# Moving the SBUF buffers of a two-model fp32 kernel: starts at multiples of 64 bytes, and different offsets modulo 512 bytes

## The chip, the cores and the metric

The kernel runs on one core of one Trainium2 chip. The metric is the device time of one execution in microseconds; the median of three runs is given for the kernel before.

## What is computed

Two small transformer-like blocks are run one after the other on one sequence of 512 tokens with 1024 channels, all in fp32. Cut to what matters, each of the linear layers is `h @ w` with 1024 (or 2816) rows of weights:

```python
for layer in range(2):                       # first block
    h = rmsnorm(x, attn_norm[layer])
    x = x + (even_mixer if layer == 0 else odd_mixer)(h, ...)   # projections, attention, output projection
    x = x + conv_glu_ffn(rmsnorm(x, ffn_norm[layer]), ...)      # 1024 -> 2 x 2816 -> 1024
x = rmsnorm(x, final_norm)
for i in range(2):                           # second block
    h = _rmsnorm(x, norm_g) * (1 + scale) + shift
    proj = h @ w_in                          # queries, keys, indexer, gates, state-space inputs
    merged = sigmoid(gl_att) * y_att + sigmoid(gl_ssd) * y_ssd
    x = x + gate * (merged @ w_out)
return rmsnorm(x, final_g)
```

## The kernel before, in words

Activations lie transposed in SBUF: 128 channels on the partitions, 512 tokens along the free axis, so a vector of 1024 channels is 8 tiles of 128 x 512 fp32 (2048 bytes in each partition). `xT` is the residual stream, `hT` the normalised input of a layer, and `arena` is one large buffer from which every stage takes its temporaries by an `Area`, in whole numbers of words from the arena's start. `arena_r` and `hv_r` are the same memory as `arena` and `hv`, seen as the type that TensorE reads in one pass (F32R).

**Linear layers.** To keep fp32 accuracy, a weight tile and an activation tile are each split into a high part and a low part, and a product is made of three matmuls: high by high, high by low, low by high (`pe_linear_steps`, `pe_pair`; all recorded at line 458 in the helper `mm`). A matmul is 128 x 128 weights (the stationary operand, loaded by a weight load of its own) by 128 x 512 activations (the moving operand). The weights arrive in panels of eight tiles, 512 KB each: SP moves panel after panel into the five slots of `ring`. ACT copies a panel's high part into one of three slots of `wparts` (line 566), then DVE, or POOL for some panels, subtracts and writes the low part (line 570). This is `keep_up`, which each engine calls in its own program so that it stays two panels ahead of TensorE; `tile_of` gives TensorE the next weight tile and waits for the low part. A slot of `wparts` is written again when TensorE has finished the panel three back, a slot of `ring` when its low part is made.

The activation operand of a linear layer is either `hT` (its high and low halves) or a pair of tiles in the arena: the attention output, the gated hidden channels of the feed-forward layer, the state-space output and the merged gates are split there by ACT (line 596) and DVE (line 600). The bf16 matmuls of `pe_busy` (line 533, recorded at 458) only keep TensorE working while a norm is computed.

**Order.** Each engine has its own program; semaphores tie them. The order of the matmuls is written out by hand, and nothing in it depends on an address.

**Where the buffers lie.** Buffers are laid one behind the other, each rounded up to 32 bytes in a partition. The first, `ring`, begins at byte 16512. From the sizes, before and after the change (the byte within a partition, then that byte modulo 64 and modulo 512):

| buffer | before | mod 64 | mod 512 | after | mod 64 | mod 512 |
|---|---|---|---|---|---|---|
| ring | 16512 | 0 | 128 | 16896 | 0 | 0 |
| wparts slots 0, 1, 2 | 36992, 45184, 53376 | 0 | 128, 128, 128 | 37376, 45632, 54016 | 0 | 0, 64, 256 |
| xT | 61568 | 0 | 128 | 62208 | 0 | 256 |
| hT high, low | 77952, 94336 | 0 | 128, 128 | 78592, 95040 | 0 | 256, 320 |
| hv, rot, vecs | 110720, 118912, 123008 | 0 | 128 | 111424, 119616, 123712 | 0 | 320 |
| cf_sb | 125088 | 32 | 160 | 125824 | 0 | 384 |
| cb_sb | 128928 | 32 | 416 | 129664 | 0 | 128 |
| small, rstd, arena | 131040, 132064, 136160 | 32 | 480 | 131776, 132800, 136896 | 0 | 192 |

`vecs` has 517 columns, 2068 bytes, which take 2080; that is what puts everything behind it at 32 modulo 64. The tiles that the linear layers read in the arena begin at multiples of 64 bytes from its start, so in the kernel before they lie at 480 or at 32 modulo 512.

Of the kernel before, what the change touches and what calls it, by code (L numbers as in the profile page):

```python
# [8 lines left out]
F32 = mybir.dt.float32  # L9
F32R = mybir.dt.float32r  # L10
BF16 = mybir.dt.bfloat16
ALU = mybir.AluOpType
ACT = mybir.ActivationFunctionType
AX = mybir.AxisListType

P = 128
D = 1024
KD = D // P
SEQ = 512
# [13 lines left out]
RAW = 5  # L33
PARTS = 3
# [106 lines left out]
def vec_layout():  # L141
    at, n = {}, 0
    for name, layer, cols in (
        [("attn_norm", l, KD) for l in range(2)] + [("ffn_norm", l, KD) for l in range(2)]
        + [("conv_w", (l, j), FC) for l in range(2) for j in range(3)] + [("conv_b", l, FC) for l in range(2)]
        + [("final_norm", 0, KD), ("pos_k", 0, CMP_LEN), ("pos_v", 0, CMP_LEN), ("b_f", 0, 1), ("c", 0, KD)]
        + [("b_ada", l, 24) for l in range(2)] + [("norm_g", l, KD) for l in range(2)]
        + [("xconv_w", (l, j), 12) for l in range(2) for j in range(4)] + [("xconv_b", l, 12) for l in range(2)]
        + [("dt_bias", l, 1) for l in range(2)] + [("a_log", l, 1) for l in range(2)]
        + [("d_skip", l, KD) for l in range(2)] + [("ssm_g", l, KD) for l in range(2)] + [("final_g", 0, KD)]  # L150
    ):
        at[name, layer] = n
        n += cols
    return at, n


VEC, NVEC = vec_layout()
# [89 lines left out]
def finish(steps):  # L247

    if isinstance(steps, STEPS_TYPE):
        for _ in steps:  # L250
            pass
# [102 lines left out]
def build(nc, ins, out, known=None, final=False):  # L354
    stream_of, x_in, vec_in, cf_in, cb_in, rot_in = ins
# [8 lines left out]
    with ExitStack() as ctx:  # L364
        def sb(name, shape, dt=F32):
            return ctx.enter_context(nc.sbuf_tensor(name, shape, dt))

        ring = sb("ring", [P, RAW, KD, P])
        wparts = sb("wparts", [P, PARTS, 2, KD, P], F32R)
        xT = sb("xT", [P, KD, SEQ])  # L370
        hT = sb("hT", [P, 2, KD, SEQ], F32R)
        hv = sb("hv", [P, 4, SEQ])
        hv_r = nc.alloc_sbuf_tensor_at("hv_r", [P, 4, SEQ], F32R, offset=nc.sbuf_base - 16 * SEQ)
        rot = sb("rot", [P, 2, SEQ])
        vec = sb("vecs", [P, NVEC])
        cf = sb("cf_sb", [P, NCF])
        cb = sb("cb_sb", [P, NCB], BF16)
        small = sb("small", [P, 256])
# [24 lines left out]
        vec_landed = ctx.enter_context(nc.semaphore("vec_landed"))  # L403
# [69 lines left out]
        def landed(eng, panel):  # L473
            eng.wait_ge(panel_landed[panel % RAW], 16 * (panel // RAW + 1))

        def tile_of(pe):

            while kinds[tile_no[0] // KD] == "DVE":
                tile_no[0] += KD
            t = tile_no[0]  # L480
            tile_no[0] += 1
            panel, j = divmod(t, KD)
            ends = panel if j == KD - 1 else None
            if kinds[panel] == "split":
                if j == 0:
                    pe.wait_ge(*(pool_made if panel in lo_on_pool else dve_made)["w_lo", panel])
                slot = place[panel] % PARTS
                return (wparts[:, slot, 0, j, :], wparts[:, slot, 1, j, :]), ends
            if j == 0:
                landed(pe, panel)  # L490
            return ring[:, panel % RAW, j, :], ends
# [6 lines left out]
        def pe_linear_steps(pe, key, n, rhs, rows, ready, pool=ALL_BANKS):  # L498

            bank = banks.take(pe, (key, n), pool)  # L500
            for k in range(rows):
                (hi, lo), ends = tile_of(pe)
                if ready:
                    pe.wait_ge(*ready(k))
                last = k == rows - 1
                mm(pe, bank[:, :], lhsT=hi, rhs=rhs[:, 0, k, :], start=(k == 0), stop=False)
                mm(pe, bank[:, :], lhsT=hi, rhs=rhs[:, 1, k, :], start=False, stop=False)
                mm(pe, bank[:, :], lhsT=lo, rhs=rhs[:, 0, k, :], start=False, stop=last,
                   done=(key, n) if last else None, ends=ends)
                if k in (2, 5):  # L510
                    yield
            banks.panel_of[key, n] = (tile_no[0] - 1) // KD

        def pe_pair(pe, keys, rhs, ready, busy=0):
            taken = [banks.take(pe, key) for key in keys]
            pe_busy(pe, taken[0], busy)
            first = tile_no[0]
            for k in range(KD):
                pe.wait_ge(*ready(k))
                for m, (key, bank) in enumerate(zip(keys, taken)):  # L520
                    tile_no[0] = first + KD * m + k
                    (hi, lo), ends = tile_of(pe)
                    last = k == KD - 1
                    mm(pe, bank[:, :], lhsT=hi, rhs=rhs[:, 0, k, :], start=(k == 0), stop=False)
                    mm(pe, bank[:, :], lhsT=hi, rhs=rhs[:, 1, k, :], start=False, stop=False)
                    mm(pe, bank[:, :], lhsT=lo, rhs=rhs[:, 0, k, :], start=False, stop=last,
                       done=key if last else None, ends=ends)
            for m, key in enumerate(keys):
                banks.panel_of[key] = first // KD + m
# [19 lines left out]
        def keep_up(eng, who, key, ahead=PARTS - 1):  # L549

            if banks.last_panel is None:
                return
            end = banks.last_panel[key]
            upto = place[end] + ahead
            while split_at[who] <= min(upto, len(splits) - 1):
                i = split_at[who]
                p = splits[i]
                if any(k != "split" for k in kinds[end + 1:max(end, p - RAW) + 1]):
                    return
                split_at[who] += 1  # L560
                slot = i % PARTS
                if who == "act":
                    landed(eng, p)
                    if i >= PARTS:
                        eng.wait_ge(*filled["panel", splits[i - PARTS]])
                    eng.activation(wparts[:, slot, 0, :, :], ring[:, p % RAW, :, :], ACT.Copy)\  # L566
                       .then_inc(*act_made.mark(("w_hi", p)))
                elif (who == "pool") == (p in lo_on_pool):
                    eng.wait_ge(*act_made["w_hi", p])
                    eng.tensor_tensor(wparts[:, slot, 1, :, :], ring[:, p % RAW, :, :],  # L570
                                      wparts[:, slot, 0, :, :].bitcast(F32), ALU.subtract)\
                       .then_inc(*(pool_made if who == "pool" else dve_made).mark(("w_lo", p)))

        HALF = slice(0, DH), slice(DH, P)
# [2312 lines left out]
        @block.sync  # L2887
        def _(sp):
            for t in range(NT):
                sp.dma_start(x_nat[:, t, :], x_in[t * P:(t + 1) * P, :]).then_inc(x_landed[t], 16)  # L2890
            for i in range(n_panels):
                if i >= RAW:
                    old = i - RAW
                    kind = kinds[old]
                    lo_made = pool_made if old in lo_on_pool else dve_made
                    sp.wait_ge(*(lo_made["w_lo", old] if kind == "split" else filled["panel", old] if kind == "PE"
                                 else dve_made["ada panel", old]))
                sp.dma_start(ring[:, i % RAW, :, :].rearrange("p k w -> p (k w)"), stream_of[i])\
                  .then_inc(panel_landed[i % RAW], 16)
                if i == 1:  # L2900
                    sp.dma_start(cf[:, P:NCF], cf_in[:, P:NCF]).then_inc(cf_landed, 16)
                if i == 2:
                    sp.dma_start(cb[:, :], cb_in).then_inc(cb_landed, 16)
                    sp.dma_start(rot[:, :, :].rearrange("p a b -> p (a b)"), rot_in[:, 0:2 * SEQ]).then_inc(rot_landed, 16)

            sp.wait_ge(*dve_made["y last"])
            for t in (0, 2, 1, 3):
                sp.wait_ge(*(act_made if t < 2 else dve_made)["y", t])
                sp.dma_start(out[t * P:(t + 1) * P, :], y_nat[:, t, :]).then_inc(out_stored, 16)
            sp.wait_ge(out_stored, 16 * NT)  # L2910

        @block.scalar
        def _(act):
            act.dma_start(cf[:, 0:P], cf_in[:, 0:P]).then_inc(ident_landed, 16)
            act.dma_start(vec[:, :], vec_in).then_inc(vec_landed, 16)
            for part in prog["act"]:
                finish(part(act))

# [93 lines left out]
```

## Time and profile before

| | |
|---|---|
| median of 3 runs | 2462.91 us (2462.30 to 2463.08) |
| profiled execution, span from the first to the last instruction | 2462.0 us |
| TensorE matmuls | 12086, busy 97% of the span |
| of these, 128 x 512 by weights in `wparts` | 5520 + 48 with hT as the moving operand, 2400 with the arena |
| DVE, ACT, POOL busy | 58%, 41%, 11% |
| mean granted TensorE clock | 0.990 |

The profiled execution's own time beyond the span is not given; its span lies 0.9 us under the median of the runs. Busy time of TensorE is the union of the matmuls' intervals; since they are pipelined, the mean duration of one (some 390 ns) is longer than the distance from one start to the next. That distance is had from a merged stretch of the timeline: (its length minus the duration of the last one) divided by the count minus one.

### The profile page before, as it was taken

The page shows a single profiled execution, that of the slowest core. Times are in us where ns is not written, and L with a number is a line of the kernel's source. Part 1 is how long each engine was busy: PE and PEld are TensorE (multiplying, and loading weights), DVE is VectorE, ACT ScalarE, POOL GpSimd, SP SyncE. Part 2 cuts the span into 40 slices and gives each one's busy share as a digit, 9 for nine tenths or more (in the row PEclk, how much of TensorE's full clock was granted, in tenths as well). Part 3 has the DMA queues.
Part 4 walks back from the last instruction along what each step waited for, and adds up shares of the span by engine and source line. Part 5 has one row for each costly group of instructions (what it writes and reads, how often), then busy time and mean ns, then how long its engine had stood idle before and what let it go on. Part 6 is the DMA issues. An engine that isn't in the chain of part 4 may idle for free.

```text
span 2462.0 us, 32019 instructions
## 1 busy us (share of the span) xinstructions
PE 2394.7 (97%) x12086; PEld 1926.7 (78%) x12086; DVE 1423.4 (58%) x2366; ACT 1019.3 (41%) x1732; POOL 273.9 (11%) x260
## 2 busy tenths in 40 slices
PE   8999899999999999999999999989999999999998
PEld 7877788888887888788888866767888777678886
DVE  3545665655655666566556469947533578666333
ACT  3666664322334444443233334444422354445223
POOL 0000111000000000100000236302100233011001
PEclk8999999999999999999999999999999999999999
DMA  4311002433432111133433312101222221102321
GB/s 180 111 52 44 1 27 95 153 122 128 151 123 87 66 54 61 52 120 130 146 127 137 112 65 73 61 35 38 94 99 91 78 74 60 43 27 78 103 95 52
DMA packets 58039, 211.77 MB, mean 86 GB/s; under 512 B 6432, under 2 KB 6560, under 8 KB 57888
## 3 DMA queue, kind: packets, MB, share of 16 engines
q1 hardware_dynamic: 57456, 208.86, 23.9%
q8 instruction: 99, 1.62, 0.3%
q10 hardware_dynamic: 432, 0.85, 0.1%
q14 instruction: 52, 0.43, 0.1%
HBM read 207.60 MB, written 2.10 MB: 85 GB/s over the span
## 4 chain that ended last, share of the span: by engine, by line
PE 84%; DVE 6%; issue 4%; ACT 3%; POOL 1%; DMA 0%; SPq 0%; ACTq 0%; DVEq 0%; POOLq 0%
PE bank L458 77%; PE last_bank L458 5%; PE bank L468 3%; DVE arena L1145 1%; DVE arena L2232 1%; DVE arena L2234 1%; DVE small L831 1%; ACT arena L819 1%; ACT wparts L566 1%; POOL rstd L625 0%; DMA cb_sb<-cb_dram 0%; DVE wparts L570 0%; DVE arena L2567 0%; DVE arena_r L584 0%; DVE arena L1006 0%
## 5 line engine op out<-in xcount | busy, mean ns | idle before, releaser
L458 PE MATMUL bank<-hT,wparts 128*128 128x512 f32 x5520 | 1335.8, 398 | 5.2 <-DMA cb_sb<-cb_dram 3.6
L458 PEld LDWEIGHTS bank<-hT,wparts 128*128 128x128 f32 x5520 | 1034.2, 190 | 237.4 <-issue 23.2
L570 DVE TENSOR_TENSOR wparts<-ring,wparts 128x1024 fp32r<-128x1024 f32 x290 | 366.7, 1265 | 427.1 <-ACT wparts L566 426.9
L458 PE MATMUL bank<-arena_r,wparts 128*128 128x512 f32 x2400 | 566.1, 396 | 0.0
L458 PEld LDWEIGHTS bank<-arena_r,wparts 128*128 128x128 f32 x2400 | 450.0, 188 | 108.5 <-DVE arena_r L600 0.3
L566 ACT ACTIVATE wparts<-ring 128x1024 fp32r<-128x1024 f32 x332 | 348.2, 1049 | 163.8 <-PE bank L458 132.6
L819 ACT ACTIVATE arena<-bank,small 128x128 f32<-128x128 f32 (+3 forms) x192 | 100.9, 526 | 143.4 <-DVE small L831 142.2
L468 PE MATMUL bank<-cf_sb,arena 128*128 128x128 f32 (+1 forms) x816 | 131.5, 278 | 14.9 <-DMA cf_sb<-cf_dram 5.2
L458 PE MATMUL last_bank<-arena 128*128 128x64 f32 x972 | 131.5, 271 | 8.6 <-DVE arena L854 4.4
L458 PEld LDWEIGHTS last_bank<-arena 128*128 128x128 f32 x972 | 122.6, 193 | 17.6 <-issue 11.4
L831 DVE TENSOR_REDUCE small<-bank 128x1 f32<-128x128 f32 (+3 forms) x192 | 93.3, 486 | 57.1 <-PE bank L458 55.0
L570 POOL TENSOR_TENSOR wparts<-ring,wparts 128x1024 fp32r<-128x1024 f32 x42 | 101.1, 2410 | 212.1 <-ACT wparts L566 212.0
L468 PEld LDWEIGHTS bank<-cf_sb,arena 128*128 128x128 f32 (+1 forms) x816 | 95.6, 146 | 30.6 <-DMA cf_sb<-cf_dram 5.2
L596 ACT ACTIVATE arena_r<-arena 128x512 fp32r<-128x512 f32 x68 | 42.9, 632 | 179.9 <-POOL arena L2791 93.7
L625 POOL TENSOR_TENSOR rstd<-hv 128x512 f32<-128x512 f32 x6 | 7.8, 1297 | 939.8 <-ACT hv L615 939.8
L458 PE MATMUL bank<-arena 128*64 128x128 f32 (+6 forms) x708 | 91.6, 330 | 14.0 <-ACT arena L819 13.5
L811 ACT ACTIVATE arena<-bank 128x384 f32<-128x384 f32 (+3 forms) x136 | 58.0, 426 | 110.5 <-PE bank L468 109.7
L1136 ACT ACTIVATE arena<-arena,vecs 128x512 f32<-128x512 f32 x44 | 36.0, 817 | 147.2 <-DVE arena L1821 147.2
L458 PEld LDWEIGHTS bank<-arena 128*128 128x128 f32 (+2 forms) x708 | 63.4, 170 | 29.6 <-ACT arena L819 16.2
L1145 DVE SCALAR_TENSOR_TENSOR arena<-arena,vecs 128x511 f32<-128x511 f32 x88 | 66.0, 750 | 16.7 <-ACT arena L1136 15.1
L458 PE MATMUL bank<-cb_sb 128*128 128x128 bf16 (+2 forms) x377 | 73.9, 253 | 0.0
L1821 DVE TENSOR_TENSOR arena<-bank,rstd 128x512 f32<-128x512 f32 x44 | 30.4, 691 | 66.5 <-PE bank L458 62.1
(277 smaller groups left out, 2125.5 us busy)
## 6 DMA issues: line engine op xcount, KB each, us to landing
ring<-weights_dram SPq DMA_DIRECT2D x388, 512.0 KB, 3.3
arena<-x_dram SPq DMA_DIRECT2D x4, 512.0 KB, 6.1
out_dram<-arena SPq DMA_DIRECT2D x4, 512.0 KB, 4.0
rot<-rot_dram SPq DMA_DIRECT2D x1, 512.0 KB, 10.9
rot<-rot_dram ACTq DMA_DIRECT2D x1, 512.0 KB, 3.0
cf_sb<-cf_dram SPq DMA_DIRECT2D x1, 416.0 KB, 9.3
cb_sb<-cb_dram SPq DMA_DIRECT2D x1, 264.0 KB, 10.1
vecs<-vec_dram ACTq DMA_DIRECT2D x1, 258.5 KB, 6.1
```

What stands on the lines that cost most here:

```text
L458: i = pe.matmul(*args, **kw)
L468: i = pe.transpose(*args)
L566: eng.activation(wparts[:, slot, 0, :, :], ring[:, p % RAW, :, :], ACT.Copy)\
L570: eng.tensor_tensor(wparts[:, slot, 1, :, :], ring[:, p % RAW, :, :], wparts[:, slot, 0, :, :].bitcast(F32), ALU.subtract)\
L596: act.activation(dst, src, ACT.Copy).then_inc(*act_made.mark((key, "hi")))
L811: act.activation(PT[:, j % 3, 0:W], banks[key, "t", j][:, 0:W], ACT.Copy)\
L819: act.activation(Pb[:, i % 3, 0:W], banks[key, "s", i][:, 0:W], ACT.Exp, bias=mx(i), accum_out=sm(i)).then_inc(*act_made.mark((key, "p", i)))
L831: dve.tensor_reduce(mx(i), banks[key, "s", i][:, 0:W], AX.X, ALU.max, negate=True)\
L1136: act.activation(cv, src, ACT.Identity, bias=b, scale=w).then_inc(*act_made.mark((key, "tap", n)))
L1145: dve.scalar_tensor_tensor(out=cv[:, s:SEQ], in0=src[:, 0:SEQ - s], scalar=w, in1=cv[:, s:SEQ], op0=ALU.mult, op1=ALU.add)\
L1821: dve.tensor_tensor(an[:, n % 3, :], banks[(key, "a"), n][:, :], scale, ALU.mult)\
L2232: dve.max(tops[:, r, :], sc).then_inc(*dve_made.mark((K + "top", qt, r)))
```

## The change

It puts padding buffers ahead of `ring`, ahead of the second and third slot of `wparts` (which become three buffers) and between the two halves of `hT` (which become two buffers in a `Pair`, indexed as before), and rounds `vecs` up to 528 columns. The padding is never read or written. No instruction is added or removed, no shape, no order and no wait is changed; the DMA into `vecs` writes the same 517 columns.

```diff
--- before.py
+++ after.py
@@ -365,14 +365,21 @@
         def sb(name, shape, dt=F32):
             return ctx.enter_context(nc.sbuf_tensor(name, shape, dt))
 
+        sb("pad_ring", [P, 96])
         ring = sb("ring", [P, RAW, KD, P])
-        wparts = sb("wparts", [P, PARTS, 2, KD, P], F32R)
+        wparts = []
+        for i in range(PARTS):
+            if i:
+                sb(f"pad_w{i}", [P, (0, 16, 48)[i]])
+            wparts.append(sb(f"wparts{i}", [P, 2, KD, P], F32R))
         xT = sb("xT", [P, KD, SEQ])
-        hT = sb("hT", [P, 2, KD, SEQ], F32R)
+        hi_of_h = sb("hT_hi", [P, KD, SEQ], F32R)
+        sb("pad_h", [P, 16])
+        hT = Pair(hi_of_h, sb("hT_lo", [P, KD, SEQ], F32R))
         hv = sb("hv", [P, 4, SEQ])
         hv_r = nc.alloc_sbuf_tensor_at("hv_r", [P, 4, SEQ], F32R, offset=nc.sbuf_base - 16 * SEQ)
         rot = sb("rot", [P, 2, SEQ])
-        vec = sb("vecs", [P, NVEC])
+        vec = sb("vecs", [P, (NVEC + 15) // 16 * 16])
         cf = sb("cf_sb", [P, NCF])
         cb = sb("cb_sb", [P, NCB], BF16)
         small = sb("small", [P, 256])
@@ -485,7 +492,7 @@
                 if j == 0:
                     pe.wait_ge(*(pool_made if panel in lo_on_pool else dve_made)["w_lo", panel])
                 slot = place[panel] % PARTS
-                return (wparts[:, slot, 0, j, :], wparts[:, slot, 1, j, :]), ends
+                return (wparts[slot][:, 0, j, :], wparts[slot][:, 1, j, :]), ends
             if j == 0:
                 landed(pe, panel)
             return ring[:, panel % RAW, j, :], ends
@@ -563,12 +570,12 @@
                     landed(eng, p)
                     if i >= PARTS:
                         eng.wait_ge(*filled["panel", splits[i - PARTS]])
-                    eng.activation(wparts[:, slot, 0, :, :], ring[:, p % RAW, :, :], ACT.Copy)\
+                    eng.activation(wparts[slot][:, 0, :, :], ring[:, p % RAW, :, :], ACT.Copy)\
                        .then_inc(*act_made.mark(("w_hi", p)))
                 elif (who == "pool") == (p in lo_on_pool):
                     eng.wait_ge(*act_made["w_hi", p])
-                    eng.tensor_tensor(wparts[:, slot, 1, :, :], ring[:, p % RAW, :, :],
-                                      wparts[:, slot, 0, :, :].bitcast(F32), ALU.subtract)\
+                    eng.tensor_tensor(wparts[slot][:, 1, :, :], ring[:, p % RAW, :, :],
+                                      wparts[slot][:, 0, :, :].bitcast(F32), ALU.subtract)\
                        .then_inc(*(pool_made if who == "pool" else dve_made).mark(("w_lo", p)))
 
         HALF = slice(0, DH), slice(DH, P)
@@ -2912,7 +2919,7 @@
         @block.scalar
         def _(act):
             act.dma_start(cf[:, 0:P], cf_in[:, 0:P]).then_inc(ident_landed, 16)
-            act.dma_start(vec[:, :], vec_in).then_inc(vec_landed, 16)
+            act.dma_start(vec[:, 0:NVEC], vec_in).then_inc(vec_landed, 16)
             for part in prog["act"]:
                 finish(part(act))
 
```

## Rows read from the trace of the kernel before

**Rows 1.** The page: span, busy time by engine, PE's slices and its granted clock
```profile
span 2462.0 us, 32019 instructions
...
PE 2394.7 (97%) x12086; PEld 1926.7 (78%) x12086; DVE 1423.4 (58%) x2366; ACT 1019.3 (41%) x1732; POOL 273.9 (11%) x260
...
PE   8999899999999999999999999989999999999998
...
PEclk8999999999999999999999999999999999999999
```

**Rows 2.** The page: the chain that ended last, by engine and by line
```profile
PE 84%; DVE 6%; issue 4%; ACT 3%; POOL 1%; DMA 0%; SPq 0%; ACTq 0%; DVEq 0%; POOLq 0%
PE bank L458 77%; PE last_bank L458 5%; PE bank L468 3%; DVE arena L1145 1%; DVE arena L2232 1%; DVE arena L2234 1%; DVE small L831 1%; ACT arena L819 1%; ACT wparts L566 1%; POOL rstd L625 0%; DMA cb_sb<-cb_dram 0%; DVE wparts L570 0%; DVE arena L2567 0%; DVE arena_r L584 0%; DVE arena L1006 0%
```

**Rows 3.** Groups of PE matmuls, shapes apart: busy us, mean ns | idle before
```profile
L458 PE MATMUL bank<-hT,wparts 128*128 128x512 f32 x5520 | 1335.8, 398 | 5.2 <-DMA cb_sb<-cb_dram 3.6 <-DVE arena L1145 0.9 <-POOL wparts L570 0.6
L458 PE MATMUL bank<-arena_r,wparts 128*128 128x512 f32 x2400 | 566.1, 396 | 0.0
L458 PE MATMUL last_bank<-arena 128*128 128x64 f32 x972 | 131.5, 271 | 8.6 <-DVE arena L854 4.4 <-DVE arena L857 0.9 <-ACT arena L811 0.6
...
L458 PE MATMUL last_bank<-hT,wparts 128*128 128x512 f32 x48 | 12.9, 411 | 0.0
```

**Rows 4.** Timeline of PE, 1797 to 1848: start, us to last end, instructions
```profile
1797.24 11.06 PE L458 MATMUL bank<-hT,wparts 128*128 128x512 f32 x48
1808.14 11.38 PE L458 MATMUL bank<-arena_r,wparts 128*128 128x512 f32 x48
1819.35 11.05 PE L458 MATMUL bank<-hT,wparts 128*128 128x512 f32 x48
1830.24 5.76 PE L458 MATMUL bank<-arena_r,wparts 128*128 128x512 f32 x24
1835.84 11.06 PE L458 MATMUL bank<-hT,wparts 128*128 128x512 f32 x48
```

**Rows 5.** Timeline of PE, a long stretch with a right operand in the arena
```profile
1176.51 61.78 PE L458 MATMUL bank<-arena_r,wparts 128*128 128x512 f32 x264
```

**Rows 6.** Timeline of PE, back-to-back bf16 matmuls of 512 columns
```profile
1423.07 3.41 PE L458 MATMUL bank<-cb_sb 128*128 128x512 bf16 x15
```

**Rows 7.** Timeline of PE, a short run inside the third stage (forgetting attention)
```profile
906.20 1.78 PE L458 MATMUL bank<-hT,wparts 128*128 128x512 f32 x7
```

**Rows 8.** Tile wparts, PE and its weight loads: ns min/median/max
```profile
L458 PEld LDWEIGHTS bank<-hT,wparts x5520: 186/188/333, 15.1 to 2396.6; 128*128 128x128 f32 x198
...
L458 PEld LDWEIGHTS bank<-arena_r,wparts x2400: 186/188/192, 350.8 to 2449.7; 128*128 128x128 f32 x185
...
L458 PE MATMUL bank<-hT,wparts x5520: 387/389/796, 15.1 to 2396.8; 128*128 128x512 f32 x198
...
L458 PE MATMUL bank<-arena_r,wparts x2400: 388/394/482, 350.8 to 2450.0; 128*128 128x512 f32 x185
```

**Rows 9.** Tile arena_r, PE: matmuls with weights in the arena
```profile
L458 PE MATMUL bank<-arena_r x160: 222/337/481, 243.8 to 999.5; 128*128 128x128 f32 x40, 128*128 128x256 f32 x40, 128*128 128x384 f32 x40, 128*128 128x512 f32 x40
L458 PE MATMUL bank<-hv_r,arena_r x64: 221/336/741, 72.1 to 235.7; 128*128 128x128 f32 x16, 128*128 128x256 f32 x16, 128*128 128x384 f32 x16, 128*128 128x512 f32 x16
```

**Rows 10.** Groups of ACT and DVE instructions, shapes apart (two answers, ACT first)
```profile
L566 ACT ACTIVATE wparts<-ring 128x1024 fp32r<-128x1024 f32 x332 | 348.2, 1049 | 163.8 <-PE bank L458 132.6 <-DMA ring<-weights_dram 31.2
L596 ACT ACTIVATE arena_r<-arena 128x512 fp32r<-128x512 f32 x68 | 42.9, 632 | 179.9 <-POOL arena L2791 93.7 <-DVE arena L1830 86.2
...
L615 ACT ACTIVATE hv<-xT 128x512 f32<-128x512 f32 x48 | 29.9, 623 | 92.1 <-DVE xT L2852 31.1 <-DVE xT L1116 30.9 <-DVE xT L1112 30.1
...
L570 DVE TENSOR_TENSOR wparts<-ring,wparts 128x1024 fp32r<-128x1024 f32 x290 | 366.7, 1265 | 427.1 <-ACT wparts L566 426.9
L1732 DVE SCALAR_TENSOR_TENSOR arena<-ring,small,arena 128x1024 f32<-128x1024 f32 x42 | 53.7, 1279 | 0.0
```

**Rows 11.** Who waited for whom: us in total, times, longest us
```profile
DVE wparts L570 <- ACT wparts L566: 426.9, 263, 5.3
...
ACT wparts L566 <- PE bank L458: 132.6, 43, 4.6
...
ACT wparts L566 <- DMA ring<-weights_dram: 31.2, 7, 12.2
```

**Rows 12.** The page: DMA issues, KB each, median us to landing
```profile
ring<-weights_dram SPq DMA_DIRECT2D x388, 512.0 KB, 3.3
...
vecs<-vec_dram ACTq DMA_DIRECT2D x1, 258.5 KB, 6.1
```

## The prediction

> **What bounds the kernel now.** I read the page first. TensorE has a matmul in flight for 97% of the span, and no slice of the 40 falls far below that; the granted clock reads 8 tenths in the first slice and 9 (90% or more of 2.4 GHz) in every other [rows 1]. The chain that ended last is TensorE's for 84% of the span, DVE has 6%, ACT 3% and DMA 0% [rows 2]. So only what shortens or lengthens matmuls counts in full. Next the groups by shape: three quarters of TensorE's busy time is one kind of instruction, 128 x 512 activations against a 128 x 128 weight tile from `wparts`: 5520 + 48 of them with `hT` moving, 2400 with the arena moving [rows 3]. The mean durations (398 and 396 ns) hide the difference that matters here, because they hold the pipeline's latency and, for hT, stretches with interruptions. The timeline shows it. In one stage of the second model the two kinds alternate in equal stretches: 48 matmuls on hT take 11.06 us from first start to last end, 48 on the arena take 11.38 [rows 4]. Take off the duration of the last, 389 and 394 ns [rows 8], and divide by 47: **227.0 ns from start to start on hT, 233.7 on the arena**. The long stretch says the same: (61.78 - 0.39) / 263 = 233.4 ns [rows 5]. Same weights' buffer, same shape, same type, no idle time; what differs is where the moving operand lies: hT at 0 modulo 64, the arena at 32 modulo 64, by the address table.
>
> 512 columns at 2.4 GHz are 213.3 ns. The bf16 filler matmuls come near: (3.41 - 0.38) / 14 = 216.4 ns [rows 6], with 0.38 for the duration of one [rows 3]. They also lie at 32 modulo 64 and pay nothing visible, but they read half the bytes in the same time. So the fp32 stream at one column a cycle seems to be at the edge of what its reads deliver. In round numbers the two are 544 and 560 cycles at 2.4 GHz, 226.7 and 233.3 ns, which I use from here; the difference of 16 cycles, 6.67 ns, is the time of 16 columns, that is of 64 bytes. A row of 2048 bytes at 32 modulo 64 touches 33 pieces of 64 bytes, an aligned one 32. That fits one extra piece for each arena matmul; it is an inference, the trace shows no addresses.
>
> **The change part by part.**
>
> *The arena at a multiple of 64.* 2400 matmuls go from 233.3 to 226.7 ns: 2400 x 6.67 = **16.0 us** less. All of it is on TensorE's chain: the group has 0.0 us of idle time before it [rows 3]. The cover that must hold is the making of weight parts. A panel is 24 matmuls, 24 x 226.7 = 5.4 us (5.6 before on the arena); in it DVE needs 1.27 us and ACT 1.05 for the parts [rows 10], and the next panel lands in 3.3 us [rows 12]. DVE and ACT wait for each other and for TensorE, hardly for the DMA, 31.2 us in seven waits [rows 11]. So nothing is late next, and I charge 0; if the cover went, the price would be at most the 0.2 us a panel that was gained, 100 arena panels x 0.2 = 16 us, the whole gain.
>
> *Other matmuls that read the arena or cf_sb.* TensorE's other busy time is 2394.7 - 1335.8 - 566.1 - 12.9 = 480 us [rows 1, 3]. Most are two-instruction fp32 products or short ones, the largest 972 of 64 columns, 131.5 us [rows 3]; they don't read at the full rate. The one-pass products with weights in the arena give the nearest direct comparison: with `arena_r` moving (misaligned) the minimum and median are 222 and 337 ns, with `hv_r` moving (aligned) 221 and 336 [rows 9], a difference of 1 ns; but there the weights are misaligned in both, and the runs are three matmuls long. Bounds: 0, and 480 x 6.7 / 226.7 = 14 us if all of it scaled as the arena stretches do. By the nearest row, 1 ns in 337, I take 1.5 us.
>
> *ACT, DVE, POOL.* ACT's copy of 512 columns takes 632 ns from and to the arena, and a square from xT to hv, both aligned, 623; DVE's two-source operation of 1024 columns takes 1279 in the arena and 1265 on ring and wparts [rows 10]. The operations differ too, so 1 to 1.5% is the upper bound of the gain from alignment. They are on the chain for 9% of the span, 222 us [rows 2]: 0 to 3 us, I take 1. Off the chain it is hidden by TensorE.
>
> *hT and the weights.* They are aligned already. What the change moves is the distance between the two streams that TensorE reads at once, the moving rows and the next weights (a weight load takes 188 ns of the 227, so it runs beside the matmul [rows 8]). Before, hT and every weight slot are both at 128 modulo 512, distance 0; the arena is at a distance of 352 or 416. After, the distance is 256 or 320, 192 or 256, and 0 or 64, for the three slots. The trace of before has no aligned pair at a distance other than 0. The bounds: at best the excess over the bf16 distance of 216.4 vanishes, 227 to 216.4 ns, 5568 x 10.6 = 59 us on hT and 2400 x 10.3 = 25 us more on the arena; at worst distance 0 is what makes hT cheap, and hT goes to the arena's 233.4, 5568 x 6.7 = 37 us lost. There is also a middle: in short runs the distance is not settled, (1.78 - 0.39) / 6 = 231.7 ns in a run of seven [rows 7], against 227.0 in long ones [rows 4]; the same addresses, so something of the two streams' timing matters. I take 0: the arena's excess over hT is explained by one piece of 64 bytes at distances of 352 and 416, with nothing left over for the distance, so the value nearest to the rows is no effect.
>
> The page on TensorE of the Trainium skill ("TensorE: Matmul & The Clock Gate", Part 2) says that the engine has two independent read ports, and that loading the next weights steals nothing from the running matmul. By it the distance is worth nothing in either direction, as I took it; 227 against 216.4 ns is not explained by it.
>
> *Padding, vecs, DMA.* 736 bytes more in a partition; no engine works on them. The panel DMAs have the same packets and a destination 384 bytes further, hidden by the ring's depth; the vecs DMA lands the same bytes in 6.1 us [rows 12]. 0.
>
> The sum: 16.0 + 1.5 + 1 = 18.5 us less. 2462.0 - 18.5 = 2443.5 as a span; with the 0.9 us by which the median of the runs stands above it, **2444.4 us**.
>
> **The rivals.**
>
> 1. *The distance matters and gets better* (chance 0.25). For: the 11 ns above the bf16 rate, and the unsettled 231.7 ns [rows 4, 6, 7]. Against: distances of 0, 352 and 416 show the same once the extra piece is taken off. Price: half of the excess, 5 ns for 7968 matmuls, is 40 us on top: 2404. The full excess gives 2444 - 84 = 2360. Nearer ones, such as all runs settling at 226.7, give 5 to 10 us, 2437.
>
> 2. *Distance 0 was the cheap place* (chance 0.17; slower). The trace can't tell "aligned" from "at the same offset modulo 512 as the weights", since hT has both and the arena neither. If the second is what gives 227 ns, all 5568 hT matmuls go towards 233.4, and the arena stays: 2463 + 37 = 2500. If alignment is right and the distance costs as well, say as in the unsettled run, hT goes to 231.7 for + 5568 x 4.7 = 26 us, the arena gains 4: 2485. It decides from a loss of 2.9 ns for each hT matmul on (16 / 5568). Against: at 352 and 416, two different distances, the arena's excess is the same, and it is just one piece of 64 bytes.
>
> 3. *Nothing changes* (chance 0.12). If the reads are made in pieces smaller than 64 bytes, 32 modulo 64 is no misalignment and the 6.7 ns come from something that stays, as the place in the arena or the way its tiles follow each other. Then 2462. The hv_r against arena_r rows, 1 ns apart [rows 9], speak for it; the two clean levels of rows 4 and 5 speak against it, with nothing else between them. The page "SBUF — State Buffer" of the Trainium skill (Door 1, the note on cachelines) gives lines of 16 bytes; by it a start at 32 modulo 64 costs nothing, so this is the result it would have. No row shows such lines.
>
> **How the numbers follow.** Forecast as worked out, 0.46; rivals 0.25, 0.17, 0.12. Its own range is 2430 to 2447: with the upper bounds of the other matmuls and engines (14 and 3 us for 1.5 and 1) it is 2430, with neither 2447. The range of 8 in 10 takes in rival 3 and the likelier half of rival 1, to 2404, and the first 5 us of rival 2: 2404 to 2468; left out are the rest of rival 2 and the deeper half of rival 1, with the weight nearer 0.04 there. A measurement of this kernel can tell 0.2%, 4.9 us, from no change. Faster by more than that: 0.46 + 0.25 = 0.71. Within: rival 3, and 0.01 of rival 2 in which its loss just balances the gain, 0.13. Slower: the rest of rival 2, 0.16.
>
> **What would show it.** Right: the stretches of 48 arena matmuls [rows 4] take 11.06 us, the stretch of 264 takes 60.0 instead of 61.78, hT stretches still 11.06. Rival 1: hT stretches of 48 below 10.9 us. Rival 2: hT stretches at 11.2 to 11.38. Rival 3: both as before. ACT's 632 ns going to 623 would show the third term by itself. I would be wrong in kind if the three weight slots came out different from one another, panel by panel, for then the distance counts and the mean hides it.

## The result, and the profile after

The changed kernel takes **2478.75 us** (median of 4 runs, 2477.25 to 2479.52) against 2462.61 for the kernel before; the ratio is 1.0065, with a 95% interval of 1.0053 to 1.0077. It is 16 us slower where 18.5 us faster was forecast, and lies outside the stated range of 2404 to 2468.

The page of the changed kernel, span, busy time, clock and chain (it answers to [rows 1, 2]):

```profile
span 2476.7 us, 32007 instructions
...
PE 2408.3 (97%) x12074; PEld 1921.2 (78%) x12086; DVE 1424.0 (57%) x2366; ACT 1019.8 (41%) x1732; POOL 273.9 (11%) x260
...
PEclk9999999999999999999999999999999999999999
...
PE 83%; DVE 7%; issue 4%; ACT 4%; POOL 1%; DMA 0%; SPq 0%; ACTq 0%; DVEq 0%; POOLq 0%
```

TensorE still bounds the kernel, with 13.6 us more of busy time; DVE, ACT and POOL have what they had. (The trace holds 12 matmul records fewer, all of bf16 matmuls on `cb_sb`; the program has the same matmuls.) The groups of matmuls by shape (busy us, mean ns | idle before); hT is now two buffers, whose intervals overlap, so their busy times can't be added:

```profile
L465 PE MATMUL bank<-hT_hi,wparts 128*128 128x512 f32 x3680 | 1221.2, 403 | 5.1 <-ACT hT_hi L700 4.2 <-DVE rstd L2353 0.4 <-DVE hT_lo L745 0.4
L465 PE MATMUL bank<-hT_lo,wparts 128*128 128x512 f32 x1840 | 729.1, 396 | 0.0
L465 PE MATMUL bank<-arena_r,wparts 128*128 128x512 f32 x2400 | 561.9, 394 | 0.0
```

Against [rows 3], 2400 arena matmuls take 561.9 us instead of 566.1. The high half of hT has 403 ns for the mean of one, the low half 396, 398 before for both. The timeline, in the stage of [rows 4] (of the hT stretches the first row alone stands here, since the two halves alternate):

```profile
1805.21 5.71 PE L465 MATMUL bank<-arena_r,wparts 128*128 128x512 f32 x24
1810.76 0.40 PE L465 MATMUL bank<-hT_hi,wparts 128*128 128x512 f32 x1
...
1821.90 11.18 PE L465 MATMUL bank<-arena_r,wparts 128*128 128x512 f32 x48
1832.91 0.39 PE L465 MATMUL bank<-hT_hi,wparts 128*128 128x512 f32 x1
...
1844.09 5.66 PE L465 MATMUL bank<-arena_r,wparts 128*128 128x512 f32 x24
```

A stretch on hT lasts from its first start to the start of the arena stretch behind it: 1821.90 - 1810.76 = 11.14 us for 48, **232.1 ns**, and 1844.09 - 1832.91 = 11.18, 232.9. In [rows 4] the same was 1808.14 - 1797.24 = 10.90, 227.1. The arena stretches went from 11.38 to 11.18 and from 5.76 to 5.71 and 5.66. And the long one, [rows 5] 61.78 us:

```profile
1182.95 61.66 PE L465 MATMUL bank<-arena_r,wparts 128*128 128x512 f32 x264
```

(61.66 - 0.39) / 263 = 233.0 ns: it lies at a multiple of 64 now and has gained 0.4 ns of the 6.7. Where the forecast had 60.0 us, nearly nothing happened. The tiles' rows (duration ns min/median/max, first and last start), which answer to [rows 8], show the loss in the durations as well:

```profile
L465 PE MATMUL bank<-hT_hi,wparts x3680: 387/395/803, 14.8 to 2412.2; 128*128 128x512 f32 x194
...
L465 PE MATMUL bank<-arena_r,wparts x2400: 387/394/483, 347.7 to 2464.6; 128*128 128x512 f32 x185
...
L465 PE MATMUL bank<-hT_lo,wparts x1840: 387/396/632, 15.1 to 2411.9; 128*128 128x512 f32 x184
```

The median on hT was 389 ns and is 395 and 396, the arena's is 394 as it was. From the first to the last arena matmul it was 2099.2 us and is 2116.9.

To see which matmuls pay, I took each distance from one start to the next out of the trace, for all consecutive pairs of 128 x 512 matmuls with weights in `wparts`, and averaged those up to 262 ns (longer ones hold a wait, or ran at the lower of the two granted clocks, 1.2 GHz). The trace has no addresses: each matmul's come from the kernel's program, whose order of matmuls is the trace's. A pair is counted by its earlier matmul, and the distance from weight to moving operand is taken modulo 256:

```
                                 count, after   before    after
hT                                      5115    227.9    232.6
  slot 0 (after: 0 high, 64 low)        1633    227.8    231.9
  slot 1 (after: 192 high, 0 low)       1848    227.9    233.8
  slot 2 (after: 0 high, 64 low)        1634    227.9    231.9
arena                                   2377    233.5    231.7
  after, tiles at distance 0             563              228.4
  after, tiles at distance 128           416              232.3
  after, tiles at distance 192          1398              232.8
```

5100 x 4.7 = 24 us are lost on hT and 2380 x 1.8 = 4.3 gained on the arena: 20 us at 2.4 GHz, where the two spans differ by 14.7. The rest is the clock. The two profiled executions did not have the same:

```profile
core 0: 2462.0 us, clock 0.990
```

```profile
core 0: 2476.7 us, clock 0.992
```

By the trace, the kernel before was at 1.2 GHz for 48.3 us of its span and the changed one for 37.5. Of the pairs on hT, 73 ran at 1.2 GHz before, at 430 ns in the mean, and 37 after. Those that were longer than 262 ns at 2.4 GHz, which are the ones with a wait, sum to 75.8 us before and 75.9 after, so no part of the loss went into waits. At 430 ns instead of 228 a stretch does about half the work: 10.8 / 2 = 5.4 us came back, an estimate, and 20 - 5.4 = 14.6.

The other terms of the sum: ACT and the waits around the weight parts (two views; they answer to [rows 10, 11]):

```profile
L603 ACT ACTIVATE arena_r<-arena 128x512 fp32r<-128x512 f32 x68 | 42.9, 631 | 178.7 <-POOL arena L2798 92.6 <-DVE arena L1837 86.2
...
L622 ACT ACTIVATE hv<-xT 128x512 f32<-128x512 f32 x48 | 29.9, 624 | 90.6 <-DVE xT L2859 30.5 <-DVE xT L1119 30.1 <-DVE xT L1123 30.1
```

```profile
DVE wparts L577 <- ACT wparts L573: 431.0, 263, 5.6
...
ACT wparts L573 <- PE bank L465: 131.3, 41, 4.8
...
ACT wparts L573 <- DMA ring<-weights_dram: 31.4, 6, 12.7
```

ACT's 632 ns in the arena are 631, 623 are 624: alignment to 64 bytes gives ACT nothing.

### The profile page after: what moved, and what is told of

It reads as the page before. It is cut to its first block, busy times and chain, and to the rows that moved or that the text cites. A ratio compares the mean times of both kernels' runs of the same rounds, so it can differ in the third digit from the quotient of the medians.

```text
span 2476.7 us, 32007 instructions
## 1 busy us (share of the span) xinstructions
PE 2408.3 (97%) x12074; PEld 1921.2 (78%) x12086; DVE 1424.0 (57%) x2366; ACT 1019.8 (41%) x1732; POOL 273.9 (11%) x260
## 4 chain that ended last, share of the span: by engine, by line
PE 83%; DVE 7%; issue 4%; ACT 4%; POOL 1%; DMA 0%; SPq 0%; ACTq 0%; DVEq 0%; POOLq 0%
PE bank L465 76%; PE last_bank L465 4%; PE bank L475 3%; DVE arena L1152 1%; DVE arena L2239 1%; DVE arena L2241 1%; ACT wparts L573 1%; DVE small L838 1%; ACT arena L826 1%; POOL rstd L632 0%; DVE arena L2574 0%; DVE wparts L577 0%; DMA ring<-weights_dram 0%; ACT arena L2147 0%; DVE arena L2226 0%
## 5 line engine op out<-in xcount | busy, mean ns | idle before, releaser
L465 PE MATMUL bank<-hT_hi,wparts 128*128 128x512 f32 x3680 | 1221.2, 403 | 5.1 <-ACT hT_hi L700 4.2
L465 PEld LDWEIGHTS bank<-hT_hi,wparts 128*128 128x128 f32 x3680 | 695.5, 189 | 180.0 <-issue 16.6
L465 PE MATMUL bank<-hT_lo,wparts 128*128 128x512 f32 x1840 | 729.1, 396 | 0.0
L465 PE MATMUL bank<-arena_r,wparts 128*128 128x512 f32 x2400 | 561.9, 394 | 0.0
L465 PEld LDWEIGHTS bank<-hT_lo,wparts 128*128 128x128 f32 x1840 | 348.0, 189 | 78.5 <-issue 6.2
L475 PE MATMUL bank<-cf_sb,arena 128*128 128x128 f32 (+1 forms) x816 | 129.9, 276 | 14.7 <-DMA cf_sb<-cf_dram 5.0
L465 PEld LDWEIGHTS last_bank<-arena 128*128 128x128 f32 x972 | 124.0, 195 | 16.9 <-issue 10.6
L465 PE MATMUL bank<-arena 128*64 128x128 f32 (+6 forms) x708 | 92.0, 331 | 14.1 <-ACT arena L826 13.6
```

Source lines behind the costliest of these rows:

```text
L465: i = pe.matmul(*args, **kw)
L475: i = pe.transpose(*args)
```

## The experiments

Three theories stood after this. **D**: what is cheap is a moving operand at the same offset, modulo 256 or 512, as the weights (rival 2 of the prediction, in general form). **A**: alignment to 64 bytes, as forecast, with something else lost on top. **O**: the place in SBUF. All kernels are the kernel before with padding (e8 and e11 also move tiles inside the arena), except e9, which is the changed kernel with one padding moved. Beside them the kernel before had medians of 2462.8 to 2463.0 us. The bytes of padding behind a moved buffer bring those after it back to their offset modulo 512. "ns" is the mean distance from start to start as above. The last column is the span times the mean granted clock of each execution, the median of them: an estimate of the span had the clock been 2.4 GHz throughout. It is there because the mean clock was between 0.9895 and 0.993 from kernel to kernel, and 0.001 of it is 2.5 us.

| run | hT to weights, mod 256 | arena to weights, mod 256 | hT ns | arena ns | median us | ratio to before, 95% | span x clock, us |
|---|---|---|---|---|---|---|---|
| before | 0 | 96, 160 | 227.9 | 233.5 | 2462.6 | | 2435 to 2437 |
| after | see above | see above | 232.6 | 231.7 | 2478.75 | 1.0053 to 1.0077 | 2456.1 |
| e1_arena_equal | 0 | 0, 64 | 227.9 | 229.0 | 2452.39 | 0.9935 to 0.9969 | 2426.3 |
| e2_round64 | 0 | 128, 192 | 227.9 | 232.6 | 2459.60 | 0.9976 to 0.9995 | 2435.8 |
| e3_h_low_64 | 0 high, 64 low | 96, 160 | 231.9 | 233.4 | 2478.69 | 1.0047 to 1.0077 | 2458.4 |
| e4_w_64 | 192 | 32, 96 | 233.2 | 233.2 | 2485.60 | 1.0076 to 1.0106 | 2464.8 |
| e5_w_128 | 128 | 224, 32 | 232.5 | 233.3 | 2482.92 | 1.0058 to 1.0090 | 2460.0 |
| e6_w_256 | 0 (256) | 96, 160 | 227.9 | 233.5 | 2462.34 | 0.9984 to 1.0002 | 2437.9 |
| e7_all_misaligned | 0 | 0, 64 | 227.9 | 229.0 | 2453.12 | 0.9943 to 0.9971 | 2425.8 |
| e8_all_equal | 0 | 0 | 227.8 | 226.9 | 2447.69 | 0.9920 to 0.9945 | 2419.3 |
| e9_after_h_together | 0, 192, 0 by slot | as after | 230.1 | 231.7 | 2468.19 | 1.0015 to 1.0034 | 2442.9 |
| e10_slots_only | 0, 192, 0 by slot | mixed | 230.1 | 233.4 | 2471.24 | 1.0024 to 1.0049 | 2446.2 |
| e12_w_32 | 224 | 64, 128 | 233.1 | 230.3 | 2479.19 | 1.0055 to 1.0081 | 2456.8 |
| e11_constants_too | 0 | 0 | 227.9 | 226.9 | 2448.67 | 0.9928 to 0.9954 | 2418.0 |

In every run the last column moved as the two "ns" columns say (5100 times the one, 2400 times the other), to within 3.3 us. e4 and e6 answer theory O: the same buffer, moved by 64 bytes, costs 23 us, and moved further, by 256, costs nothing; e7, where everything is moved by 32 bytes, has the time of e1.

**e1_arena_equal**: the arena alone moved, to the offset of the weights.

```diff
+        sb("pad_arena", [P, 40])
         arena = sb("arena", [P, ARENA])
```

> The kernel before with 160 bytes of padding ahead of the arena alone: the arena then begins at 128 modulo 512, where hT and the weight slots already are. Theory D (what is cheap is a moving operand at the same offset modulo 256 or 512 as the weights): the arena matmuls whose tiles are at 128 go from 233.4 to about 226.7 ns; the third or so of them in the second model whose tiles lie 64 bytes further (at 192) stay at 232 to 234. 1570 x 6.7 ns = 10.5 us less, 2452. Theory A (alignment to 64 bytes, any distance): all 2400 gain, 16 us, 2446.5. hT matmuls as before, 227.9 ns in the mean, by both. Theory O (the offset from the start of SBUF or the place in it matters, not the relation): no change.

Measured: 2452.4, as theory D had it. The tiles at distance 0 came to 227.5 ns, those 64 bytes further to 231.9. In the timeline of the stage of [rows 4], whose arena tiles are mostly the latter, the gain is accordingly small, 11.38 to 11.36:

```profile
1801.57 11.36 PE L459 MATMUL bank<-arena_r,wparts 128*128 128x512 f32 x48
1812.76 11.08 PE L459 MATMUL bank<-hT,wparts 128*128 128x512 f32 x48
1823.68 5.76 PE L459 MATMUL bank<-arena_r,wparts 128*128 128x512 f32 x24
```

**e2_round64**: the alignment alone.

```diff
-        vec = sb("vecs", [P, NVEC])
+        vec = sb("vecs", [P, (NVEC + 15) // 16 * 16])
...
-            act.dma_start(vec[:, :], vec_in).then_inc(vec_landed, 16)
+            act.dma_start(vec[:, 0:NVEC], vec_in).then_inc(vec_landed, 16)
```

> The alignment alone: vecs rounded up to 528 columns and nothing else, so the arena, cf_sb, small and rstd begin at multiples of 64 bytes, the arena at 0 modulo 512 and so 384 (and 448) away from the weights at 128. Theory A: arena matmuls at 226.7 ns, 16 us less, 2446.5. Theory D: arena matmuls stay between 231 and 234 ns, time within 0.2% of before, 2458 to 2464.

```profile
1805.87 11.31 PE L458 MATMUL bank<-arena_r,wparts 128*128 128x512 f32 x48
1817.02 11.06 PE L458 MATMUL bank<-hT,wparts 128*128 128x512 f32 x48
1827.92 5.71 PE L458 MATMUL bank<-arena_r,wparts 128*128 128x512 f32 x24
```

Theory A falls: the arena at a multiple of 64 has 11.31 us for 48 where A wants 11.06. The arena matmuls at 128 and 192 are 0.9 ns below those at 96 and 160, 2400 x 0.9 = 2.2 us. The median is 3 us lower, but the mean granted clock was 0.9913 against 0.9898, which is more than that, and the span times the clock shows no gain; so the 3 us can't be put down to the alignment.

**e3_h_low_64**: the split of hT alone.

```diff
-        hT = sb("hT", [P, 2, KD, SEQ], F32R)
+        hi_of_h = sb("hT_hi", [P, KD, SEQ], F32R)
+        sb("pad_h", [P, 16])
+        hT = Pair(hi_of_h, sb("hT_lo", [P, KD, SEQ], F32R))
+        sb("pad_back", [P, 112])
```

> The kernel before with only the low half of hT moved, by 64 bytes (448 bytes of padding behind it keep all later buffers at their offsets modulo 512). Theory D in its strict form (all three products of a tile must be at distance 0 for the stream to settle): hT matmuls at about 231.5 ns in the mean instead of 227.9, 5100 x 3.6 = 18 us more, 2480. In its loose form (each product pays for itself): only the third of them that moves the low half pays, 6 us more, 2468. Theory A: no change.

Measured: 2478.7, 16 us more, as much as the whole change (23 in span times clock, against its 20). The tile's rows (duration ns min/median/max):

```profile
L461 PE MATMUL bank<-hT_hi,wparts x3680: 387/395/797, 14.9 to 2413.3; 128*128 128x512 f32 x194
...
L461 PE MATMUL bank<-hT_lo,wparts x1840: 387/395/629, 15.5 to 2413.0; 128*128 128x512 f32 x184
```

The high half did not move and is at distance 0, yet its median is 395 ns, as the low half's, where the row of before has 389 [rows 8]: the strict form holds. One product of three at another distance takes the other two with it: by their starts, 232.0 ns for the high half and 231.7 for the low.

**e4_w_64**, **e5_w_128**, **e6_w_256**, **e12_w_32**: the weight slots together moved by 64, 128, 256 and 32 bytes (the second padding is 112, 96, 64 and 120 words).

```diff
+        sb("pad_w", [P, 16])
         wparts = sb("wparts", [P, PARTS, 2, KD, P], F32R)
+        sb("pad_back", [P, 112])
         xT = sb("xT", [P, KD, SEQ])
```

> The kernel before with all three weight slots moved by 64 bytes together (192 modulo 512) and nothing else. Theory D: hT matmuls lose distance 0 and go to 231 to 234 ns, 18 to 30 us more, 2481 to 2493, the arena ones stay near 233. Theory A: no change. If the different offsets of the three slots were what cost in the changed kernel, moving them together costs nothing.

> The weight slots alone moved by 128 bytes, to 256 modulo 512; hT at 128. Theory D with a modulus of 128: hT stays at 227.9, 2463. With a modulus of 256 or 512: hT at 231 to 233 ns, 2480 to 2487. The changed kernel had arena tiles at a distance of 128 at 232.3 ns, which speaks for the second.

> The weight slots alone moved by 256 bytes, to 384 modulo 512; hT at 128. Theory D with a modulus of 256: hT stays at 227.9 ns, 2463 (the changed kernel had arena tiles at a distance of 256 at 228.5 ns). With a modulus of 512: hT at 231 to 233, 2480 to 2487.

> The weight slots alone moved by 32 bytes, to 160 modulo 512. Tells how exact the equality must be. If a distance within one piece of 64 bytes is as good as none, hT stays at 227.9 and the time at 2463; if it must be exact, hT at 231 to 233 and 2480 to 2487, as at 64 and at 128 bytes.

The timelines in the stage of [rows 4], in the order 64, 128, 256, 32; 48 on hT took 11.06 before:

```profile
1798.91 11.35 PE L460 MATMUL bank<-hT,wparts 128*128 128x512 f32 x48
1810.11 5.74 PE L460 MATMUL bank<-arena_r,wparts 128*128 128x512 f32 x24
1815.68 11.35 PE L460 MATMUL bank<-hT,wparts 128*128 128x512 f32 x48
```

```profile
1811.07 11.31 PE L460 MATMUL bank<-hT,wparts 128*128 128x512 f32 x48
1822.22 11.37 PE L460 MATMUL bank<-arena_r,wparts 128*128 128x512 f32 x48
```

```profile
1802.55 11.38 PE L460 MATMUL bank<-arena_r,wparts 128*128 128x512 f32 x48
1813.76 11.05 PE L460 MATMUL bank<-hT,wparts 128*128 128x512 f32 x48
```

```profile
1807.11 11.36 PE L460 MATMUL bank<-hT,wparts 128*128 128x512 f32 x48
1818.31 11.31 PE L460 MATMUL bank<-arena_r,wparts 128*128 128x512 f32 x48
```

11.35, 11.31, 11.05 and 11.36: the modulus is 256, and 32 bytes off is as bad as 64 or 128. In e12 the arena came down by 3 ns, to 229.2 for its tiles at distance 64 and 232.4 at 128, which is where its time is 6 us below e4's. hT's low half at 64 had 231.7 in e3, the arena in e1 231.9; so among the unequal ones the distance modulo 256 is not all that counts. Modulo 512 these distances are not the same, 64 in e1 and e3, 320 in e12, but e1's belong to other tiles in another model; no run separates the two, and this part stays open.

**e7_all_misaligned**: e1 with everything 32 bytes further.

```diff
+        sb("pad_ring", [P, 8])
         ring = sb("ring", [P, RAW, KD, P])
...
+        sb("pad_arena", [P, 40])
         arena = sb("arena", [P, ARENA])
```

> As e1, but with 32 bytes of padding ahead of ring, so that weights, hT, hv and the arena all lie at 160 modulo 512, that is at 32 modulo 64: equal to one another and all off the multiple of 64. Theory D: as e1, hT at 227.9 and the arena's distance 0 tiles at 227.5 ns, 2452. Theory A (a start off the multiple of 64 costs one more read for each matmul): hT goes to 233.3, the arena back to 233.4, 2490.

```profile
1168.07 60.00 PE L460 MATMUL bank<-arena_r,wparts 128*128 128x512 f32 x264
```

```profile
1809.94 11.08 PE L460 MATMUL bank<-hT,wparts 128*128 128x512 f32 x48
```

The long arena stretch of [rows 5], 61.78 us, takes 60.00, and 48 on hT take 11.08, with both operands of these matmuls at 32 modulo 64. That is the counterpart of e2: equal and off the boundary is fast, on the boundary and unequal is not.

**e8_all_equal**: e1, and the tiles of the second model moved inside the arena.

```diff
+        sb("pad_arena", [P, 40])
         arena = sb("arena", [P, ARENA])
...
             wi = A.take(NT, 4)
+            A.at += P - NT * 4
             xbc_at = A.at
```

> As e1, and in the second model the tiles behind the 16 words of wi are moved up by 112 words inside the arena, so that every activation tile of a linear layer lies at 128 modulo 512, as the weights do. Theory D: all 2400 arena matmuls at about 227.5 ns, another 820 x 4.4 = 3.6 us less than e1: 2449. If the equality that e1 made was not what gave its gain, the tiles moved here stay at 232 ns and the time at 2452.

The timeline in the same stage, and the groups:

```profile
1799.36 11.04 PE L459 MATMUL bank<-arena_r,wparts 128*128 128x512 f32 x48
1810.24 11.04 PE L459 MATMUL bank<-hT,wparts 128*128 128x512 f32 x48
1821.12 5.60 PE L459 MATMUL bank<-arena_r,wparts 128*128 128x512 f32 x24
```

```profile
L459 PE MATMUL bank<-hT,wparts 128*128 128x512 f32 x5520 | 1335.4, 398 | 5.2 <-DMA cb_sb<-cb_dram 4.1 <-DVE arena L1146 1.0
L459 PE MATMUL bank<-arena_r,wparts 128*128 128x512 f32 x2400 | 550.5, 390 | 0.0
```

48 matmuls take 11.04 us now, whether on the arena or on hT, and the arena group 550.5 us instead of 566.1. At **2447.7 us, ratio 0.9933 (0.9920 to 0.9945)**, it is faster than both kernels.

**e9_after_h_together** and **e10_slots_only**: the other half of the change undone, and done alone.

```diff
         hi_of_h = sb("hT_hi", [P, KD, SEQ], F32R)
-        sb("pad_h", [P, 16])
         hT = Pair(hi_of_h, sb("hT_lo", [P, KD, SEQ], F32R))
+        sb("pad_h", [P, 16])
```

```diff
-        wparts = sb("wparts", [P, PARTS, 2, KD, P], F32R)
+        wparts = []
+        for i in range(PARTS):
+            if i:
+                sb(f"pad_w{i}", [P, (0, 16, 48)[i]])
+            wparts.append(sb(f"wparts{i}", [P, 2, KD, P], F32R))
+        sb("pad_back", [P, 64])
```

> The changed kernel with the 64 bytes between the halves of hT moved behind the low half: both halves at 256 modulo 512, the slots still at 0, 64 and 256, the arena at 192. Theory D with modulus 256: hT matmuls with the weights of slots 0 and 2 (distances 256 and 0) go back to 227.9 ns, those of slot 1 (192) to 232 or 233; mean 229.5 instead of 232.6, 5100 x 3.1 = 16 us less than the changed kernel, 2463; the arena as in the changed kernel, 231.7. If the split of the halves was not what unsettled slots 0 and 2, time and hT matmuls stay as in the changed kernel, 2479.

> The kernel before with the three slots at different offsets alone (128, 192 and 384 modulo 512), everything else where it was modulo 512. Theory D with modulus 256: slots 0 and 2 stay at 227.9 on hT, slot 1 (distance 448) goes to 233.2 as in the run with all slots at that distance; 1750 x 5.3 = 9 us more, 2472. If differing slots are a cost by themselves (the change of slot every 24 matmuls), all three rise and it is 2480 or more.

By slot, 0, 1, 2: 227.9, 233.3, 228.7 ns in e9 and 227.9, 233.2, 228.7 in e10. Slot 1 pays, slot 0 does not, slot 2 a little: its panels come behind slot 1's. In e10 an unbroken panel in slot 2 behind one in slot 1 had 227.9 ns, one in slot 0 behind slot 2 had 226.7; before the change both had 226.7. In e10's timeline three stretches of 48 on hT take

```profile
1805.60 11.09 PE L463 MATMUL bank<-hT,wparts 128*128 128x512 f32 x48
...
1827.72 11.21 PE L463 MATMUL bank<-hT,wparts 128*128 128x512 f32 x48
...
1844.37 11.24 PE L463 MATMUL bank<-hT,wparts 128*128 128x512 f32 x48
```

11.09, 11.21 and 11.24 us: the panels of the first are in slots 2 and 0, those of the other two in slots 0 and 1. e10 met its 2472. e9 is 10.6 us below the changed kernel where 16 were expected; the mean on hT is 230.1 ns instead of the expected 229.5, which is 3 us, and the mean clock was 0.9907 against 0.9915, which is 2.

**e11_constants_too**: e8 with cf_sb, cb_sb, small, rstd at 128 modulo 256 as well.

```diff
-        sb("pad_arena", [P, 40])
...
+        sb("pad_cf", [P, 56])
         cf = sb("cf_sb", [P, NCF])
...
+        sb("pad_small", [P, 48])
         small = sb("small", [P, 256])
```

> As e8 (every activation tile of a linear layer at the weights' offset), and cf_sb, cb_sb, small and rstd also at 128 modulo 256, which puts the transposes, masks and norms on the same offset and on multiples of 64. If the pairing matters for matmuls that don't read a column a cycle as well, TensorE's other 480 us shrink by up to 1 or 2%, 5 to 10 us below e8, 2438 to 2443. If it matters only for the one-pass fp32 matmuls, 2447, as e8.

Measured: 2448.7 against e8's 2447.7, with overlapping intervals: no difference that can be told. As far as the medians show, the matmuls outside the linear layers don't care.

## Why the prediction was wrong, point by point

- **What bounds the kernel** was right. TensorE's one kind of matmul decides, and the difference of 6.7 ns between hT and the arena in [rows 4, 5] is real. Its cover was right too: when the gain was really had (e8), the panel's preparation did not become late.
- **"The arena at a multiple of 64 ... 16.0 us less"** is the step that failed first. The trace had two explanations for one difference, alignment and equality of offsets, and I took alignment, because 16 cycles are just 64 bytes' worth of columns and one more piece fits. The coincidence was numerical. Measured: 0.4 ns of 6.7 on the long stretch, and e2 and e7 separate the two. What the step promised was there to be had, by equality: e8 took 15 us, its long stretch 60.00 us as forecast. That the 16.0 us were the right size for it is no merit of the step: the price was read from the rows, and only its cause was wrong.
- **"hT and the weights ... I take 0"** is the second failure, and follows from the first: the argument was that nothing was left over for the distance once the extra piece was taken off. The row that should have carried weight is [rows 7]: with the same addresses, a run of seven had 231.7 ns and a long one 227. Equality does not make a matmul fast by itself; it lets a stream settle at 226.7. The changed hT stream has 232.6 ns, near what the unsettled run had. The term was 5100 x 4.7 = 24 us at 2.4 GHz where 0 stood. The sign that the prediction itself had given for being wrong in kind was there too: the three slots came out at 231.9, 233.8 and 231.9 ns.
- **Rival 2** was the outcome, in its milder form: it named 231.7 for hT (measured 232.6), 4 us for the arena (4.3), and a total of 2485, 6 us too much, of which 5 are the clock, as worked out above. Its arena term was met by luck: it gave the 4 us to alignment, but 563 x 5.1 = 2.9 us of them are the tiles that came to lie at distance 0. It had a chance of 0.17, and the range ended 11 us short of the result. Its counterargument, that distances of 352 and 416 show the same excess, was worth nothing: unequal is unequal. Rival 3 was right on the arena, where alignment changed nearly nothing, and its row of `hv_r` against `arena_r` [rows 9] had spoken for it.
- **The pages.** The page "TensorE: Matmul & The Clock Gate" of the Trainium skill (Part 2), by which loading the next weights takes nothing from the running matmul, does not agree with e4, e5 and e12: moving the weights alone, with everything that streams left in place, slowed the hT stream from 227.9 to 232.5 ns or more. The measurement decides. The page "SBUF — State Buffer" of the Trainium skill (Door 1, the note on cachelines) gives lines of 16 bytes, by which a start at 32 modulo 64 costs nothing. The measurements agree with that much: all off the multiple of 64 but equal (e7) had 227.9 and 229.0 ns, as on it (e1).
- **ACT, DVE** (1 us) and **the other matmuls** (1.5 us): ACT's durations did not move (631 and 624), and e11 shows no gain. DVE's two-source operation in the arena took 1279 ns at 32 modulo 64 and 1278 on the boundary. So the alignment was not what set these operations apart from the faster ones.
- **Slips in the working.** 100 panels at 0.2 us are 20 us, not 16; the 16 come with the unrounded 0.16. The 0.38 us for one bf16 matmul stands in no line of [rows 3]; the group of the filler matmuls has it (379 ns). Neither changes the forecast.

The parts, each done alone: split of hT + 15.9 us, slots + 8.3, alignment - 3.2; together + 16.1. In span times clock, the better measure here, they are + 23, + 10 and + 1, together + 20. They don't add, since the split alone already slows hT matmuls in all three slots by 4 ns, also in slot 1, the one that the slots' offsets slow. The move of `ring` was not tried alone.

## What to carry to other kernels

Where fp32 matmuls of 512 columns run one behind the other in one pass, as in this kernel, let the stationary and the moving operand begin at the same offset modulo 256 bytes, and let all products of one chain do so. Tiles whose size is a multiple of 256 bytes keep the offset of the buffer; a small allocation between them, like the 16 words of `wi`, shifts all that follow. Spreading the buffers over different offsets made this kernel slower. Other shapes and types were not measured apart.

When kernels differ by less than 1%, look at the granted clock of each execution before explaining the last few microseconds: the executions of the kernel before went from 2458.2 us at 0.993 to 2467.6 at 0.988, and the clock made the change look 4 us cheaper than the matmuls' distances say.

When two properties change together between a fast and a slow group of rows, the rows price the difference and say nothing of the cause.

## What the runs showed of the hardware that was not expected

A stream of such matmuls has memory. The distances from start to start, one by one, in a run of the kernel before that begins at 163.4 us (offsets equal), in the changed kernel from 393.2 us on (hT, slot 1), and in its arena stretch at distance 192:

```
equal, before                    235 234 236 224 231 235 229 232 231 227 226 227 227
hT, slot 1, after                235 237 226 235 239 234 236 237 226 235 239 234
arena at distance 192, after     233 233 234 233 233 234 233 233 234
```

With equal offsets the pattern runs out after nine matmuls at most in nearly all runs and stays at 226.7 ns, 544 cycles at 2.4 GHz: over the 64 unbroken hT runs of 15 distances or more in the kernel before, the first nine have a mean of 230.0 ns, the tenth 226.7. With unequal ones it goes round as long as the run lasts, here with 1407 ns for six, or stands at 233.3, 560 cycles. It is not ACT or DVE: in the kernel before, the distances on hT during which both were idle had a mean of 227.4 ns, and those during which DVE made a low part 227.3; in e4 these are 233.2 and 233.3. Equality counts modulo 256 bytes (e5, e6) and 32 bytes off is already too much, on either side (224 in e12, 233.1 ns; 32 in e4's arena, 233.1). What in the chip ties the two reads together, and why some unequal pairs (229.2 ns in e12's arena) are better than others, was not found.
